# Both down projections by Strassen's seven products, with the sums of weights and inner tiles made in place

## What is computed

```
# first block
m = rms_norm(h, mlp_norm[i])
h = h + jnp.square(jax.nn.relu(m @ w_mlp_up[i])) @ w_mlp_down[i]
gate = jax.nn.sigmoid(rms_norm(h, ple_norm[i]) @ w_ple_gate[i] + b_ple_gate[i])
h = h + (p[i] @ w_ple_proj[i]) * gate
# second block
ff = square(relu(h2 @ w_up)) @ w_down
x = x + _rmsnorm(ff, g_mlp_post)
```

## Time and profile before

| | us |
|---|---|
| median of 3 runs (2722.75 to 2726.74) | 2722.95 |
| the profiled execution, its own time | 2725.15 |
| its span, first to last instruction | 2723.5 |
| PE busy | 2587.6 |
| DVE busy | 1461.1 |
| ACT busy | 942.4 |

### The profile page before, as it was taken

How to read it: one execution, slowest core, us unless ns; L and a number is a source line. 1 busy time by engine, 2 the same in 40 slices (tenths; PEclk the granted TensorE clock), 3 DMA queues, 4 the chain that set the end, 5 groups by cost and what they waited for, 6 DMA issues and landing times.

```text
span 2723.5 us, 30576 instructions
## 1 busy us (share of the span) xinstructions
PE 2587.6 (95%) x11542; PEld 2049.2 (75%) x11542; DVE 1461.1 (54%) x1917; ACT 942.4 (35%) x1339; POOL 139.3 (5%) x253
## 2 busy tenths in 40 slices
PE   7998498999999999999999999999999999999997
PEld 6776465557888887888878877778777788888885
DVE  5235817664587773333455555445576877633336
ACT  5222135663443342111243233333355433311123
POOL 1000000000000011000001000000001000100000
PEclk9998769999999999999999999999999999999998
...
GB/s 204 42 39 20 0 0 1 1 24 139 116 113 104 124 142 167 97 104 85 46 70 162 57 47 70 62 86 139 162 117 186 108 120 105 159 97 92 93 154 109
DMA packets 70341, 256.20 MB, mean 94 GB/s; under 512 B 7616, under 2 KB 7648, under 8 KB 70192
## 3 DMA queue, kind: packets, MB, share of 16 engines
...
## 4 chain that ended last, share of the span: by engine, by line
PE 85%; DVE 7%; issue 4%; ACT 3%; DMA 1%; POOL 0%; ACTq 0%; DVEq 0%; POOLq 0%
PE ps L2086 50%; PE ps L2376 17%; PE ps L2495 7%; PE ps L2423 1%; PE ps L2441 1%; PE ps L2238 1%; PE ps L2309 1%; PE ps L2221 1%; PE ps L2235 1%; PE ps L2339 1%; DVE w_lo L1207 1%; PE ps L2319 1%; PE ps L2432 1%; DMA hA_raw<-h_spill 1%; PE ps L2245 0%
## 5 line engine op out<-in xcount | busy, mean ns | idle before, releaser
L627 ACT ACTIVATE w_hi<-w_stage 128x1024 fp32r<-128x1024 f32 x176 | 185.0, 1052 | 522.7 <-PE ps L2086 520.5
L2086 PE MATMUL ps<-hA,w_hi 128*128 128x512 f32 x1024 | 274.5, 390 | 2.4 <-DVE hA L1653 2.2
L1207 DVE TENSOR_TENSOR w_lo<-w_stage,w_hi 128x1024 fp32r<-128x1024 f32 x176 | 214.9, 1221 | 92.5 <-ACT w_hi L627 91.9
L1730 DVE TENSOR_TENSOR X<-X,ps 128x1024 f32 (+1 forms) x48 | 58.6, 1222 | 322.2 <-PE ps L2086 322.2
L2086 PEld LDWEIGHTS ps<-hA,w_hi 128*128 128x128 f32 x1024 | 191.8, 188 | 44.0 <-DVE hA L1653 3.7
L2086 PE MATMUL ps<-opP_hi,w_hi 128*128 128x512 f32 x640 | 202.5, 398 | 9.6 <-DVE w_lo L1207 8.0
L2086 PE MATMUL ps<-hB,w_hi 128*128 128x512 f32 x768 | 205.2, 389 | 0.0
L2086 PE MATMUL ps<-opP_lo,w_hi 128*128 128x512 f32 x640 | 199.4, 393 | 0.0
L2086 PE MATMUL ps<-opP_hi,w_lo 128*128 128x512 f32 x640 | 199.3, 393 | 0.0
L2086 PEld LDWEIGHTS ps<-hB,w_hi 128*128 128x128 f32 x768 | 144.2, 188 | 29.9
L2376 PE MATMUL ps<-opQ_hi,form_hi 128*128 128x512 f32 x416 | 161.8, 389 | 0.0
...
## 6 DMA issues: line engine op xcount, KB each, us to landing
w_stage<-in_w_stream SPq DMA_DIRECT2D x176, 512.0 KB, 3.5
h_spill<-T POOLq DMA_DIRECT2D x56, 512.0 KB, 3.5
pair_raw<-in_w_stream SPq DMA_DIRECT2D x26, 1024.0 KB, 5.8
hA_raw<-h_spill POOLq DMA_DIRECT2D x32, 512.0 KB, 3.6
hB_raw<-h_spill POOLq DMA_DIRECT2D x32, 512.0 KB, 3.6
g_spill<-T POOLq DMA_DIRECT2D x16, 512.0 KB, 2.9
X<-in_xT POOLq DMA_DIRECT2D x8, 512.0 KB, 10.0
...
```

The source lines that it names most:

```text
L627: act.activation(w_hi[:, slot, :], w_stage[:, slot, :], ACT.Copy).then_inc(w_hi_done, 1)
L1207: v.tensor_tensor(w_lo[:, slot, :], w_stage[:, slot, :], w_hi[:, slot, :].bitcast(F32), ALU.subtract)\
L1730: v.tensor_tensor(tile(X, n), tile(X, n), banks(2 * slot, 2), ALU.add).then_inc(evac_done, 1)
L2086: mm = pe.matmul(ps[:, psum + half, :], weight, operand[:, k, half * HALF:(half + 1) * HALF], start=(begin and x == 0 and weight is wh and ...
```

## The change

The down projection is cut in halves of the inner rows (`sc` = 0, 1; 16 inner tiles each), and within one into 2 x 2: even and odd output blocks (a), two groups of inner tiles (b) and two halves of tokens. Weights A, B, C, D and inner tiles q0 to q3 are planes of two parts of 128 x 4 x 512; each part is one DMA of 1 MB in rows of 2 KB. In place of eight products of quadrants seven are made (`Q1, Q2, Q6, Q3, Q7, Q5, Q4` in this order), each for four output blocks at once, in four banks, from 4 steps: `step` i = 0 to 27 takes 24 matmuls of 128x512, over two inner tiles. So a down projection is 56 steps of 24 = 1344 matmuls, where it was 32 blocks of 48 = 1536. `Q6` and `Q3` alternate, steps 8 to 15.

For each step ACT makes two high forms (weights W and inner tiles H, 128x1024 each, in the half of `opQ_hi` that the step before the last leaves), and DVE two low forms, in `opQ_lo`. DVE also makes the sums: S1, S3 of weights and T1, T3 of inner tiles as 128x2048 in place of a plane, S2, S4, T2, T4 as 128x1024 between the steps 7 and 15, and empties each product by `fold`: an add of four banks (128x2048) to a quadrant of `X` or to `U`, a partial sum in SBUF. The order of all this on each engine is written out by hand in `vector_steps`/`scalar_steps`, which also number the semaphores' values. The residual of x = 0 is read back in four quadrants.

Behind it, the gate of x = 0 takes the even tiles of `X` first (`gate_part`), since the odd ones get their last product from step 27 (`last_fold`), and the statistic comes behind gate block 0's odd tiles. For x = 1 there are no half blocks: the second half of tokens (h = 1) is complete after `Q5`, the first with step 27; squares, gains (now on ACT) and the scaling in pairs of tiles (`end_scale`, 128x2x512) come behind, and the output is stored in eight DMAs of 512 KB.

The core of the diff:

```diff
+Q1, Q2, Q6, Q3, Q7, Q5, Q4 = range(7)
+FIRST_STEP, LAST_STEP, STEPS = (0, 4, 8, 9, 16, 20, 24), (3, 7, 14, 15, 19, 23, 27), 28
+
+
+def form_of(i):
+
+    if 8 <= i < 16:
+        return (Q6, Q3)[i % 2], (i - 8) // 2
+    return (Q1, Q2, None, None, Q7, Q5, Q4)[i // 4], i % 4
...
-            def acc_down(b, turn, n, slot, residual=None):
-                next_low(b, turn, slot)
-                v.wait_ge(mm_done, b + 1)
-                if residual is not None:
-                    v.wait_ge(tile_landed[residual], 48)
-                v.tensor_tensor(tile(X, n), tile(X, n), banks(2 * slot, 2), ALU.add).then_inc(evac_done, 1)
...
+            def inner_in(x, sc, name, c):
+
+                b, h = {"q0": (0, 0), "q1": (0, 1), "q2": (1, 0), "q3": (1, 1)}[name]
+                row = (8 * (2 * sc + c) + 4 * b) * P
+                pool.dma_start(plane(sc, name, c), h_spill[row:row + 4 * P, h * HALF:(h + 1) * HALF].rearrange("(k p) n -> p k n", p=P))\
...
+            def forms_high(x, sc, i):
+
+                f, g = form_of(i)
+                c = g // 2
+                name_w, name_h = (("A", "q0"), ("B", "q2"), (None, None), ("B", "q3"), ("A", "q1"), ("C", "q0"), ("D", "q2"))[f]
+                last = FF_PAIRS[x] - 1
+                if sc == 0 and i < 2:
+                    act.wait_ge(ff["mm"], product_no(x, last, (0, 3)[i]))
+                else:
+                    act.wait_ge(ff["mm"], step_no(x, sc, i - 2))
+                if f in (Q1, Q2, Q4):
+                    act.wait_ge(plane_landed[name_w], plane_turn(x, sc, name_w))
+                else:
+                    act.wait_ge(ff["down"], vec_no(x, sc, {Q6: f"S2_{g}", Q3: f"S4_{g}", Q7: f"S3_{c}", Q5: f"S1_{c}"}[f]))
+                source = weight_form(ql_raw, i) if f == Q6 else weight_part(sc, name_w, g)
+                act.activation(weight_form(opQ_hi, i), source, ACT.Copy).then_inc(ff["form"], 1)
+                if f in (Q1, Q2):
+                    act.wait_ge(first_landed[name_h][c], first_turn(x, sc))
+                elif f == Q3:
+                    act.wait_ge(plane_landed[name_h], plane_turn(x, sc, name_h))
+                else:
+                    act.wait_ge(ff["down"], vec_no(x, sc, {Q6: f"T2_{g}", Q7: f"T3_{c}", Q5: f"T1_{c}", Q4: f"T4_{g}"}[f]))
...
+                v.wait_ge(ff["form"], sca_no(x, sc, f"W{i}"))
+                if f == Q6:
+                    v.wait_ge(ff["down"], vec_no(x, sc, f"S4_{g}"))
+                done(v.tensor_tensor(weight_form(opQ_lo, i), weight_form(ql_raw, i) if f == Q6 else weight_part(sc, name_w, g),
+                                     weight_form(opQ_hi, i).bitcast(F32), ALU.subtract))
+                v.wait_ge(ff["form"], sca_no(x, sc, f"H{i}"))
+                done(v.tensor_tensor(inner_form(opQ_lo, i), t2_sum[:, :, :] if f == Q6 else inner_part(sc, name_h, g),
...
+            def weight_s2(x, sc, g):
+                i = FIRST_STEP[Q6] + 2 * g
+                v.wait_ge(ff["mm"], step_no(x, sc, i - 2))
+                v.wait_ge(ff["down"], vec_no(x, sc, f"S3_{g // 2}"))
+                v.wait_ge(plane_landed["D"], plane_turn(x, sc, "D"))
+                done(v.tensor_tensor(weight_form(ql_raw, i), weight_part(sc, "D", g), weight_part(sc, "A", g), ALU.subtract))
+
+            def weight_s4(x, sc, g):
+                i = FIRST_STEP[Q6] + 2 * g
+                v.wait_ge(ff["down"], vec_no(x, sc, f"S2_{g}"))
+                done(v.tensor_tensor(weight_part(sc, "B", g), weight_part(sc, "B", g), weight_form(ql_raw, i), ALU.subtract))
...
+            def fold(x, sc, f, dst, other, settled, form=None):
+
+                v.wait_ge(ff["mm"], step_no(x, sc, LAST_STEP[f]))
+                if settled is not None:
+                    v.wait_ge(ff["down"], vec_no(x, *settled))
+                if form is not None:
+                    v.wait_ge(ff["form"], sca_no(x, 0, form))
+                done(v.tensor_tensor(dst, other, ps[:, down_bank(sc, f):down_bank(sc, f) + 4, :], ALU.add))
...
+            def down_dve(x):
+
+                x11, x12, x21, x22 = quadrant(0, 0), quadrant(0, 1), quadrant(1, 0), quadrant(1, 1)
+                for sc in range(2):
+                    plain = x == 1 and sc == 0
+                    for i in range(STEPS):
+                        f, g = form_of(i)
+                        if f == Q6:
+                            weight_s2(x, sc, g)
+                            weight_s4(x, sc, g)
+                        if f == Q3 and g == 0:
+                            if plain:
+                                fold(x, sc, Q2, x11, U[:, :, :], None, "U1")
+                            else:
+                                fold(x, sc, Q2, x11, x11, (sc, "F1a"))
+                        if f == Q3 and g:
+                            inner_t4(x, sc, g)
+                            if g < 3:
+                                inner_t2(x, sc, g + 1)
+                        if i == 16:
+                            fold(x, sc, Q6, U[:, :, :], U[:, :, :], (sc, "F1b" if sc else "F2"), None if sc else "U1")
+                        if sc or i >= 2:
...
+                        if i == 7:
+                            inner_t2(x, sc, 0)
+                            inner_t3(x, sc, 0)
...
+            def last_fold(x, m):
+
+                v.wait_ge(ff["mm"], step_no(x, 1, LAST_STEP[Q4]))
+                v.wait_ge(ff["down"], vec_no(x, 1, "V21"))
+                done(v.tensor_tensor(X[:, 2 * m + 1, 0:HALF], X[:, 2 * m + 1, 0:HALF], ps[:, down_bank(1, Q4) + m, :], ALU.add))
...
+                        pe.wait_ge(ff["down"], vec_no(x, sc, f"H{i}"))
+                        k = 4 * (i % 2)
+                        for kt in range(2):
+                            if x == 1 and sc == 1 and i == STEPS - 1 and kt == 1:
+                                pe.wait_ge(ff["down"], vec_no(1, 1, "F5b"))
+                                half_statistic(n4, 2, 0, mix_sum)
+                            for m in range(4):
+                                c = (m % 2) * 256 + kt * P
+                                wh, wl = opQ_hi[:, k + m // 2, c:c + P], opQ_lo[:, k + m // 2, c:c + P]
+                                hi, lo = opQ_hi[:, k + 2 + kt, 0:HALF], opQ_lo[:, k + 2 + kt, 0:HALF]
+                                for weight, operand in ((wh, hi), (wh, lo), (wl, hi)):
+                                    mm = pe.matmul(ps[:, down_bank(sc, f) + m, :], weight, operand,
+                                                   start=(g == 0 and kt == 0 and weight is wh and operand is hi),
+                                                   stop=(g == 3 and kt == 1 and weight is wl))
+                        mm.then_inc(ff["mm"], 1)
...
+            gate_part(B_GATE, 0)
+            gate_part(B_GATE + 1, 0)
+            gate_part(B_GATE, 1)
+            statistic(2)
+            gate_part(B_GATE + 1, 1)
+            stream(pe, B_GATE, 8, dense(opP_hi, opP_lo, None), 0, 1)
...
+            for o in range(4, DT):
+                end_add(1, o)
+            for o in range(4):
+                end_add(0, o)
+            end_scale(1, 0)
+            for o in range(4):
+                last_fold(1, o)
+            for o in range(4, DT):
+                end_add(0, o)
+            for j in range(1, 4):
+                end_scale(1, j)
+            for j in range(4):
+                end_scale(0, j)
```

708 lines of the change are left out of this document (456 added, 252 removed).

## The result

The changed kernel takes **2649.23 us** (median of 4 runs, 2647.04 to 2649.47); the kernel before, run beside it, 2723.86. The ratio is 0.9723, with an interval of 0.9706 to 0.9739. The forecast was 2646.6. The profiled execution's own time is 2649.32 and its span 2647.7, 75.8 us shorter than the span of before.

The account below looks back on a forecast made before the run. The prediction took PE (TensorE) as the bound and summed -87.1 - 4.2 + 7.8 - 3.3 + 10.4 = -76.4 us, from a median of 2722.95 to 2646.6 us; the range 2632 to 2678 left 0.15 or so outside.

Parts of the forecast that it names:

- The price of a matmul: Down stages: 384 matmuls fewer at 0.2267 us each, the pace of the profile's windows, -87.1 us.
- The old starts: Starts of both down stages: waits of 2.0 and 2.2 us with the old low parts go away, -4.2 us.
- The steps: Down stages: PE waits for DVE 1.0 us at step 8 and 0.9 at step 10 of each half, +7.8 us.
- the list: The prediction's step-by-step count of DVE operations through all 56 steps of both x, with only steps 8 and 10 late.
- Planes: Plane loads by DMA: hidden, the tightest being C with 3 us to spare, so no time added.
- the rival: Start of the down stage: plane C or D late, holding up all forms, 11 us per x, 2669 us; chance 0.08.
- Gate: Gate of x = 0, to its third block: 24.4 us against 27.7 before, -3.3 us.
- End: End of x = 1 behind PE's last issue: 30.2 us against 19.8 before, +10.4 us.
- The other sign: Down stages: ACT waiting for DVE elsewhere than in steps 8 to 15 would show the forecast wrong.
- VectorE 1.1 times as long: Steps 4 to 26: DVE is the bound, all its durations 1.1 times as long, 2668 us; chance 0.15.
- strided operands at 1.25 or more: Down stages: strided float32 operands cost DVE over 1.25 times, gain used up; at 1.3, 2742 us; chance 0.05.
- Nothing is late: Down stages and end: no step waits and the end costs +7 us, 2635 us; chance 0.10.

Follow-up runs that it names:

- Kernels 1: The changed kernel with sum T3 of the first two inner tiles made behind step 15's forms instead of step 7's: 2645.16 us.
- kernel 2: The changed kernel with T3 moved from step 7 to 15, T4 behind the Q6 steps' forms and T2 behind the Q3 steps': 2641.83 us, ratio 0.97.
- Kernel 3: The changed kernel with each inner form's low part made twice, one more VectorE operation of 1.22 us in each of 110 steps: 2717.65 us in one run.
- Kernel 4: The changed kernel with plane C of each x's first half asked for 10.9 us later, at the down stage's start: 2654.67 us in one run.

## Why the prediction was right

- **The price of a matmul.** 1344 matmuls in 308.80 us less 4.0 of waits are 0.2268 each, against 0.2267 forecast. The windows' pace was the one to use. By "Back-to-back issue gap" of the Trainium skill (TensorE: Matmul & The Clock Gate), with its 131 ns in a stream or 216 ns isolated for 512 columns, the removed matmuls would have been worth an estimated 50 or 83 us; this trace agrees with neither, since the stages became 82.5 shorter after paying about 8 of new waits and saving less than 4 of old ones.
- **The old starts.** Forecast -4.2, with the statistic taken as 0.45. The two down stages now differ by 0.98 with the same steps, so the statistic costs about 0.9 to 1.0, and some 0.5 of what I took for old waits of x=1 was the statistic: about -3.7. The trace of before agrees: by the starts its waits are 1.9 (x=0) and 1.7 us (x=1), most of it in these two rows.

```profile
1026.39 0.96 PE L2086 MATMUL ps<-hA,w_hi 128*128 128x512 f32 x3 [1.10 <-DVE hA L1653]
2359.90 0.98 PE L2086 MATMUL ps<-hA,w_hi 128*128 128x512 f32 x3 [1.11 <-DVE hA L1653]
```

- **The steps.** +7.8 forecast, 4 x 2.0 = 8.1 measured, at the two steps forecast. Kernels 1 and 2 show the mechanism by moving what stood ahead. Kernel 3 shows that at another load the list still finds the large waits but step 10's, and that it leaves out the clock.
- **Planes.** Hidden, as forecast, but my spare time was wrong: 3 us, taken from six parts at 340 GB/s, and about 8 in the trace. In the rival a plane that was 11 us late cost all of the 11. Kernel 4, with VectorE held up for 4.7 and 5.5 us, lost 3.8 and 3.3, so slack takes part of a lateness; what 11 us would cost was not run.
- **Gate.** -3.3 forecast, -2.4 measured. The last sum ended 16.9 behind the landing of step 27 (16.4 forecast), the statistic 19.0 (18.2), R 23.8 (23.0), and the third block began at 25.1 (24.4): the sums were 0.5 longer, the statistic 0.3. The rest is that I counted from the landing here and from the first gate matmul before, 0.16 apart. By the prediction's own sign a third block later than 25 us spoke against it; it was later by 0.1. The clock that this shorter wait saved, some 1.7 us, stands in no term of the sum.
- **End.** +10.4 forecast, +9.4 measured. VectorE's last operation ended 26.0 behind TensorE (26.3 forecast), the last store 3.2 later instead of 3.9.
- **The other sign.** ScalarE was to wait for VectorE in steps 8 to 15 alone. In each half it also waited, up to 3.74 us, for S1 (`spot`, L1885) ahead of the forms of steps 20 and 22. The list has S1 there, and TensorE waits at neither step, so the sign was drawn too tightly.
- **The rivals.** VectorE 1.1 times as long, and strided operands at 1.25 or more: excluded by the rows of 1.22 and 2.29. The Trainium skill (VectorE: DVE Perf Modes, Mode 1x) states that the base mode gives one result per cycle for float32 and odd strides as well, and the trace agrees. "Nothing is late" fell with the waits at steps 8 and 10; kernel 2 shows that it was within reach, for the list that I held to have "no free place" had one at step 15.

The total was 0.6 us off by the spans (75.8 against 76.4). That it is so near is luck: the parts were off by +1.0, +0.9, -1.0, +2.0 and -2.3. By the medians the forecast was 2.6 us too low: before, the profiled execution stood 2.2 above its median, and now only 0.1.
